# Output projection of a hybrid layer: token tiles 2 and 3 loaded and split in the merging stage, and half a product moved ahead of the first normalised tile

## The reference, cut to what matters

```python
merged = jax.nn.sigmoid(gate_pool) * y_pool + jax.nn.sigmoid(gate_att) * y_att
y = merged @ w_out                                        # 2048x1024 by 1024x1024
x = x + gt_m[:, None] * _rmsnorm(y, g_post_mix[layer])    # the first normalised tile: x1
h = _rmsnorm(x, g_pre_ffn[layer]) * (1.0 + sc_f[:, None]) + sh_f[:, None]
g_logits = hf @ w_group_router + b_group_router           # and the expert logits: 36 columns
```

## Time and profile before

| | us |
|---|---|
| median of 3 runs | 2522.97 (2521.85 to 2524.04) |
| the profiled execution, its own time | 2521.16 |
| its span | 2519.4 |
| PE busy in the span | 2357.6 (94%) |
| `merge`'s last matmul starts | 1317.11 |
| first matmul of `mix_out` | 1326.48 |
| first transpose of `h` | 1340.12 |

### The profile page before, as it was taken

One profiled execution on the slowest core, in us unless ns is written; L12 is line 12 of the kernel. 1 busy time (PEld: TensorE's weight loads), 2 busy tenths in 40 slices (PEclk: granted clock), 3 DMA queues, 4 the chain that ended last, 5 costly groups with the idle time before them and its releaser, 6 DMA issues. The chain is left out here.

```text
span 2519.4 us, 39603 instructions
## 1 busy us (share of the span) xinstructions
PE 2357.6 (94%) x13417; PEld 2002.0 (79%) x13418; DVE 1317.2 (52%) x1756; ACT 1001.6 (40%) x1649; POOL 482.7 (19%) x376
## 2 busy tenths in 40 slices
PE   2999999999999998998999995899999999999995
PEld 2788888887888876886777884888999989999993
DVE  7763223222111117886753456887766285656645
ACT  3400000000111105674423222787867385656655
POOL 1011110111222213100006542111122122121210
PEclk9999999999999998999999997899999999999998
DMA  7124332421446537427956433999999599787987
GB/s 267 51 67 150 134 116 85 148 67 65 156 163 232 194 140 227 165 97 237 312 177 229 155 121 138 333 350 354 315 315 290 145 326 283 242 267 236 286 284 283
DMA packets 312809, 516.61 MB, mean 205 GB/s; under 512 B 23437, under 2 KB 228773, under 8 KB 303400
## 3 DMA queue, kind: packets, MB, share of 16 engines
q1 hardware_dynamic: 282074, 418.81, 48.7%
q0 software_dynamic: 18000, 65.54, 10.2%
q10 hardware_dynamic: 12672, 31.46, 3.2%
HBM read 385.50 MB, written 130.24 MB: 205 GB/s over the span
## 5 line engine op out<-in xcount | busy, mean ns | idle before, releaser
L330 PE MATMUL proj_psum<-h_hi,proj_w_hi 128*128 128x512 f32 x1216 | 484.1, 398 | 10.7 <-DVE h_lo L432 9.6
L331 PE MATMUL proj_psum<-h_lo,proj_w_hi 128*128 128x512 f32 x1216 | 482.1, 396 | 0.0
L332 PE MATMUL proj_psum<-h_hi,proj_w_lo 128*128 128x512 f32 x1216 | 481.9, 396 | 0.0
L490 DVE COPY proj_out<-proj_psum 128x512 f32<-128x512 f32 x152 | 123.0, 813 | 598.9 <-PE proj_psum L332 598.0
L1838 PE MATMUL moe_p_gu<-moe_hi_gu,moe_xT_hi 128*128 128x256 f32 x1504 | 426.9, 284 | 1.2 <-DVE moe_xT_lo L2000 1.2
L1839 PE MATMUL moe_p_gu<-moe_lo_gu,moe_xT_hi 128*128 128x256 f32 x1504 | 422.7, 281 | 0.0
L1840 PE MATMUL moe_p_gu<-moe_hi_gu,moe_xT_lo 128*128 128x256 f32 x1504 | 422.7, 281 | 0.0
L1748 DVE TENSOR_TENSOR moe_lo_gu<-raw_gu,moe_hi_gu 128x1024 fp32r<-128x1024 f32 x256 | 302.8, 1222 | 45.7 <-ACT moe_hi_gu L1742 45.7
L1838 PEld LDWEIGHTS moe_p_gu<-moe_hi_gu,moe_xT_hi 128*128 128x128 f32 x1504 | 284.7, 189 | 3.5 <-issue 1.6
L1839 PEld LDWEIGHTS moe_p_gu<-moe_lo_gu,moe_xT_hi 128*128 128x128 f32 x1504 | 284.9, 189 | 2.1
L1840 PEld LDWEIGHTS moe_p_gu<-moe_hi_gu,moe_xT_lo 128*128 128x128 f32 x1504 | 284.7, 189 | 0.0
(11 more groups left out here) (313 smaller groups left out, 3612.2 us busy)
## 6 DMA issues: line engine op xcount, KB each, us to landing
raw_gu<-in_w_exp_gate SPq DMA_DIRECT2D x256, 256.0 KB, 6.3
raw_gu<-in_w_exp_up SPq DMA_DIRECT2D x256, 256.0 KB, 7.0
raw_d<-in_w_exp_down SPq DMA_DIRECT2D x128, 512.0 KB, 10.0
projected<-proj_out SPq DMA_DIRECT2D x38, 1024.0 KB, 4.1
proj_raw<-in_w_in SPq DMA_DIRECT2D x38, 512.0 KB, 10.8
proj_w_rest<-in_w_ada SPq DMA_DIRECT2D x8, 2048.0 KB, 9.7
y_sum<-proj_w_rest SPq DMA_DIRECT2D x20, 512.0 KB, 9.3
out_cut<-proj_cut ACTq DMA_DIRECT2D x32, 256.0 KB, 2.4
```

The lines of the kernel that those rows point to most:

```text
L330: pe.matmul(bank, w_hi[:, u, k, :], h_hi[:, k, tok], start=(k == 0), stop=False)
L331: pe.matmul(bank, w_hi[:, u, k, :], h_lo[:, k, tok], start=False, stop=False)
L332: return pe.matmul(bank, w_lo[:, u, k, :], h_hi[:, k, tok], start=False, stop=(k == KD - 1))
L490: ins = dve.tensor_copy(view[:, ds(tg * per, per), :], psum[:, u, tg, :].rearrange("p (m r) -> p m r", r=dilation))
```

## The change

Tiles 2 and 3 are loaded and split in `merge` too. Their two loads stand in SP's loop at unit 24, ahead of the store of that unit, and wait until the low parts of tiles 0 and 1 are taken, since they use the same two raw places. ACT splits them at the very end of its list in `merge`, behind the last sigmoid; POOL takes the low parts behind its weight loads, and waits for both to be done before the block ends. The multiplication of tiles 2 and 3 stays in `mix_out`.

In `mix_out` the loads, splits and low parts of tiles 2 and 3 are gone. SP's list begins with the first conditioning row; the loads of tiles 4 and 5 come behind both conditioning loads. On PE `product(2, 0)` no longer waits for a low part, and `product(3, 0)` stands ahead of `turn(0)`, where it was behind it.

```diff
-    AHEAD = 2
+    AHEAD, SPLIT_AHEAD = 2, 4
...
+                    if t >= 2:
+                        sp.wait_ge(m_lo_ready, t - 1)
                     sp.dma_start(merged_raw(pooled, t), merged.rearrange("(k p) t -> p k t", p=P)[:, :, ds(t * P, P)]).then_inc(mT_loaded[t], 16)
...
+                    if n == (CHUNKS - 1) * KD:
+                        for t in range(AHEAD, SPLIT_AHEAD):
+                            load_merged(t)
...
+                for t in range(AHEAD, SPLIT_AHEAD):
+                    pool.wait_ge(m_hi_ready, t + 1)
+                    pool.tensor_tensor(merged_tile(z_lo, t), merged_raw(pooled, t), merged_tile(z_hi, t), ALU.subtract
+                                       ).then_inc(m_late_ready, 1)
+                pool.wait_ge(m_late_ready, SPLIT_AHEAD - AHEAD)
...
+                act.wait_ge(y_summed, p_turn(UNITS - 1) + 1)
+                for t in range(AHEAD, SPLIT_AHEAD):
+                    merged_high(t)
...
-                load_merged(2)
                 sp.dma_start(mod[:, 0, :], mod_dram[0:1, 0:D].partition_broadcast(P)).then_inc(first_mod_loaded, 16)
                 load_x(0)
-                load_merged(3)
                 sp.dma_start(mod[:, 1:4, :].rearrange("p m d -> p (m d)"), mod_dram[0:1, D:4 * D].partition_broadcast(P)).then_inc(mod_loaded, 16)
+                load_merged(4)
                 load_x(1)
+                load_merged(5)
...
                 squares_y(0)
-                split(2)
                 squares_y(1)
-                split(3)
...
-                low(2)
...
-                    if t == 0:
-                        low(3)
...
                     if half == 0:
-                        pe.wait_ge(m_lo_ready, t - 1)
+                        if t >= 4:
+                            pe.wait_ge(m_lo_ready, t - 3)
                         pe.wait_ge(y_scaled, t - 1)
...
                 product(2, 0)
                 product(2, 1)
+                product(3, 0)
                 turn(0)
                 for t in range(2, TILES + 1):
-                    if t < TILES - 1:
+                    if 2 < t < TILES - 1:
                         product(t + 1, 0)
                     if t == 2:
                         route(0)
```

More of the change, by code:

```diff
@@ L894, in merge @@
         m_stored = [s.sem(f"m_stored{i}") for i in range(RP)]
-        mT_loaded = [s.sem(f"mT_loaded{i}") for i in range(AHEAD)]
+        mT_loaded = [s.sem(f"mT_loaded{i}") for i in range(SPLIT_AHEAD)]
         late_loaded = [s.sem(f"late_loaded{k}") for k in range(EARLY_K, KD)]
         (z_summed, z_hi_ready, z_lo_ready, steps, shifted, coef_exp, o_ready, o_turned, o_hi_ready, o_lo_ready, p_gated, a_gated,
-         y_summed, y_taken, m_ready, out_loaded, m_hi_ready, m_lo_ready) = (s.sem(n) for n in (
+         y_summed, y_taken, m_ready, out_loaded, m_hi_ready, m_lo_ready, m_late_ready) = (s.sem(n) for n in (
              "z_summed", "z_hi_ready", "z_lo_ready", "steps", "shifted", "coef_exp", "o_ready", "o_turned", "o_hi_ready",
-             "o_lo_ready", "p_gated", "a_gated", "y_summed", "y_taken", "m_ready", "out_loaded", "m_hi_ready", "m_lo_ready"))
+             "o_lo_ready", "p_gated", "a_gated", "y_summed", "y_taken", "m_ready", "out_loaded", "m_hi_ready", "m_lo_ready", "m_late_ready"))
         z_bank = lambda n: y[:, 0, ds((n % 2) * 512, 512)]
@@ L1253, in load_merged @@
                 def load_merged(t):
-                    if t >= 4:
-                        sp.wait_ge(m_lo_ready, t - 3)
+                    if t >= 6:
+                        sp.wait_ge(m_lo_ready, t - 5)
                     sp.dma_start(merged_raw(pooled, t), merged.rearrange("(k p) t -> p k t", p=P)[:, :, ds(t * P, P)]
@@ L1262, in load_x @@
                     sp.dma_start(xt[:, t % 2, :], x[0, ds(t * P, P), :]).then_inc(x_loaded[t % 2], 16)
-                load_merged(2)
                 sp.dma_start(mod[:, 0, :], mod_dram[0:1, 0:D].partition_broadcast(P)).then_inc(first_mod_loaded, 16)
                 load_x(0)
-                load_merged(3)
                 sp.dma_start(mod[:, 1:4, :].rearrange("p m d -> p (m d)"), mod_dram[0:1, D:4 * D].partition_broadcast(P)).then_inc(mod_loaded, 16)
+                load_merged(4)
                 load_x(1)
+                load_merged(5)
                 for t in range(2, TILES):
-                    if t + 2 < TILES:
+                    if 6 <= t + 2 < TILES:
                         load_merged(t + 2)
@@ L1279, in split @@
                 def split(t):
-                    if t >= 4:
+                    if t >= 6:
                         act.wait_ge(y_half, 2 * (t - 3))
-                    act.wait_ge(m_loaded[t % 2], 16 * (t // 2))
+                    act.wait_ge(m_loaded[t % 2], 16 * (t // 2 - 1))
                     nc.scalar.activation(merged_tile(z_hi, t), merged_raw(pooled, t), ACT.Copy).then_inc(m_hi_ready, 1)
@@ L1329, in low @@
                 def low(t):
-                    pool.wait_ge(m_hi_ready, t - 1)
+                    pool.wait_ge(m_hi_ready, t - 3)
                     pool.tensor_tensor(merged_tile(z_lo, t), merged_raw(pooled, t), merged_tile(z_hi, t), ALU.subtract
                                        ).then_inc(m_lo_ready, 1)
-                low(2)
                 for t in range(LAST + 1):
```

## The result

The changed kernel takes 2528.0 us in the median of 14 runs (2524.43 to 2530.63), the kernel before 2523.22 in 14 runs beside it (2520.61 to 2527.31). The ratio is 1.0016, 95% interval 1.0009 to 1.0023: 4.0 us slower (2.3 to 5.8). That is less than the 0.2% named as the bound of what can be told, but the interval excludes "no change". The forecast was +2.5, its range for the median 2521.5 to 2529.0.

The account below looks back on a forecast made before the run. PE, busy nearly the whole span, was taken as the bound, with one 9.0 us hole ahead of `mix_out`. 0 - 2.1 + 3.7 + 0.9 = +2.5 on 2522.97 gave 2525.5 us, range 2521.5 to 2529.0.

Parts of the forecast that it names:

- Part 1: In `merge`: two added loads and splits stay hidden behind PE's own multiplications; 0 us, upper bound 4.
- Part 2: Start of `mix_out`: conditioning row first in SP's queue lets PE start earlier; -2.1 us, bounds -3.4 to -0.7.
- Part 3: Between first and second transposes in `mix_out`: PE idles in two pieces, 1.4 and 2.2; +3.7 us, bounds 2.2 to 4.5.
- Part 4: PE's clock may fall to half in the new hole: 1.7 us at even odds, so +0.9; start stretch 0.
- the experts' 32 waits: Among the experts: transposes wait 32 times, 13.7 us in all, and the clock falls in few; evidence against a fall.
- the pattern at the end of the stage: Near the stage's end: 2.40 us idle, 1.2 us of router work at full clock, then 0.51; evidence for a fall.
- the low stretch at the start: Half clock behind the start wait of `mix_out`: expected the same as before, 0 us, bounds -1 to +1.

Follow-up runs that it names:

- Experiment 1: Changed kernel with the half product put back behind the first transposes, loads and splits staying in `merge`; ratio to the kernel before 1.0000 (0.9991 to 1.0009).
- Experiment 2: Kernel before with only the half product `product(3, 0)` moved ahead of the first transposes; ratio to the kernel before 1.0028 (1.0018 to 1.0037).
- experiment 3: Changed kernel with DVE's second scaling of h ahead of its copy of the first transposed tile; ratio to the kernel before 1.0006 (0.9995 to 1.0017).
- experiment 7: The changed kernel run once more, unedited, to see whether the clock falls again; 2528.92 us in its one run.
- experiment 6: Kernel of experiment 3 with 10 unused matmuls of 256 columns where the router waits for the copy; ratio to the kernel before 1.0006 (0.9993 to 1.0018).
- experiment 4: Changed kernel with 10 and 16 unused matmuls of 256 columns in the new hole's two pieces; ratio to the kernel before 1.0005 (0.9996 to 1.0014).
- experiment 5: Changed kernel with tile 2 in the transposes' PSUM place, products two tiles ahead, DVE's scalings earlier; ratio to the kernel before 1.0073 (1.0058 to 1.0088).
- experiment 8: Kernel of experiment 5 with DVE's choice of experts behind a scaling and the last product's halves between late transposes; 2516.67 us, ratio to the kernel before 0.9976.

## Why the prediction was right

The range held the median, near its upper end, and the direction was the one forecast. The profiled execution met one sign of failure, `merge` ending after 1317.5 (1319.04), but only by the 1.9 us that came in ahead of `merge`. By its steps:

- **Part 1, loads and splits in `merge`, 0.** Right. Last sigmoid 1304.8 where 1304.2 was worked out, low parts done at 1311.7 for 1311, no wait of PE. The sum had left out the sigmoid's own 0.64 us and put both casts ahead of the first low part, and these two slips nearly cancel. Experiment 1 shows the price of it as nothing.
- **Part 2, the start, -2.1.** Right in kind and size: start wait 6.9 against 9.0 us, released by DVE's scaling of the first product, which puts PE's start at 1324.4 when the 1.9 us are taken back. DVE went on 4.3 us after the conditioning row's issue (1320.54 to 1324.80), for the 4.4 taken from the load that had stood there. The 3.2 us estimated from the Trainium skill's figures for one transfer (DMA: Bandwidth & Descriptors, "Anatomy of one DMA") was 1.1 too short. The section fits these figures to transfers that GpSimd issues, and this one was issued by SP, with three others close behind; which of the two accounts for the difference no run here shows.
- **Part 3, the new hole, +3.7.** Right. Between the first and second transposes 6.17 us (6.2 forecast). Experiment 2 gives both waits (1.3 and 1.8 us) without the rest of the change, experiment 3 takes the second wait away by DVE's order alone. The second reads as 1.2 us in the changed kernel in place of 2.2, for two reasons. In experiments 2 and 7, where the clock fell only behind the router group, that group's row is 1.98 us and the wait 1.8; in the changed kernel it fell within the group, whose row is 2.57, 0.6 us longer, inside the hole. The other 0.4 is that the rows of transposes and router include the way through the pipeline.
- **Part 4, the clock, +0.9.** The term that was sized wrong: I took even odds of 1.7 us. In the new hole the clock fell in all three profiles with this order and cost 1.3, 1.6 and 2.0 us (experiments 2 and 7, and the changed kernel). With 2.0 the sum is 0 - 2.1 + 3.7 + 2.0 = +3.6, against 3.7 at the second router group and 4.0 at the last. I had counted the experts' 32 waits against it, but between 1594 and 2461 us, where they stand, the clock is below its full level only once, near 1734; the pattern at the end of the stage was the one that fitted. For the low stretch at the start I took 0 within 1 us either way: it was +0.2 in the changed kernel (13.84 us from the first product to the next, before 13.64), but 1.2 less in experiment 2. The prediction's reading of the Trainium skill (TensorE: Matmul & The Clock Gate, "HAM oscillation"), that waits between bursts bring the half clock back, would have given +3.3, nearer than my half of it. The traces agree that the half clock comes back in the new hole. The page's own case has longer waits than the 1.3 and 1.8 us here, so the 1.7 us were this prediction's use of it, not its figure.

That the half product stood over the chain was the whole matter: in the program of before 0.79 + 5.63 + 1.70 = 8.1 us of PE's work covered a chain of 6.2, and the change spent that cover where PE had no need of it. The last 0.3 us comes in at the end of the stage, where the waits are those of before but the clock falls sooner: the router group behind the wait of 2.46 us takes 3.63 us in the changed kernel and 2.52 before, and most of this passes inside the waits behind it:

```profile
1525.22 2.52 PE L1377 MATMUL out_p_logit<-wr,out_hT 128*128 128x36 f32 x16 [2.46 <-DVE out_hT L1425]
```

```profile
1530.83 3.63 PE L1386 MATMUL out_p_logit<-wr,out_hT 128*128 128x36 f32 x16 [2.46 <-DVE out_hT L1435]
```

## What to carry to other kernels

Before you move a piece of work to fill a wait, ask what it covers where it stands: half a product that PE does anyway is worth nothing ahead of an instruction that wasn't late, and cost 3.7 us of hole and 2 us of clock behind it. Where an engine's list is in order, an early item for the next tile behind a late one for this tile is a chain. A free PSUM place was worth more here than the earlier loads: giving tile 2 the transposes' place closed the start wait (9.4 us from merge's last matmul to the next product became 1.7; it needs tile 2 split in `merge`), while the loads and the queue order took 2 us off it. When products run further ahead, look at once for a long item in another engine's list that had slack until then, as the choice of experts had.

## What the runs showed of the hardware

The clock fell in a row of transposes, router matmuls of 36 columns and a wait of only 1.3 us (experiment 3: granted 1.00 up to 1348.8, then 0.50 for 6.8 us in which PE was busy throughout). With ten matmuls of 256 columns in place of that wait it stayed at 1.00 (experiment 6). In experiment 1, where half a product stands between the first transposes and the first router group, it stayed at 1.00 through both and the second transposes (from 1337.6 to 1346.9).

The same row (transposes, router, transposes) with neither a wait nor wide work in it was not run. The added matmuls were worth 2.0 us in the distance of experiment 4, which the ratio bears out, and 3.5 us in that of experiment 6, which it doesn't; each rests on one pair of profiles.

The attention stage, which has the same code in every kernel here, has its low stretches at different places in different executions: 3.4 us near 1007 in the kernel before, 6.8 near 1042 in the changed one, 3.4 at each place in experiment 1. Of the 7.4 us between the two profiled totals 3.4 lie outside the stages that the change touches, 1.9 ahead of them and 1.5 behind. Distances inside one execution agreed with the expectations to 0.3 us in experiments 1, 4 and 6. In experiments 2, 3, 5 and 8 they missed by 1.7 us and more, by the clock or by a chain that I hadn't seen, and the distances are what showed which.
